# One encoder step on one core: the router without a wait, half of the table products behind the first experts, later weight loads, squares summed on TensorE

## Chip, core and metric

The kernel runs on one core of a Trainium2 chip. The metric is device time in microseconds; the median of three runs of the kernel before is 1087.63 us (1087.05 to 1094.18). TensorE is called PE below, VectorE DVE, ScalarE ACT, GpSimd POOL, and SP is the engine that only issues transfers. DMA stands for the transfer engines.

## What is computed

Two layers over 288 tokens (256 of a prompt, 32 of a running stream) of width 1024, all in float32. Layer 0 mixes with RWKV-7, layer 1 with forgetting attention. Each layer has two norms, so there are norms 0 to 3; after norm 0 and norm 2 comes the mixture of 16 experts, top 2 for each token, which is where the change lies:

```python
x = _layer_norm(ALPHA * x + gt1 * y, ln_g[l, 0], ln_b[l, 0])      # norm 0, norm 2
h = x * (1 + sc2) + sh2
gl = h @ rg_w + rg_b;  el = h @ re_w + re_b                       # router
gsel = argmax(gl);  top_v, top_i = top_k(el[gsel], 2)
comb = weights of the two chosen experts
hid = silu(h @ wg[e]) * (h @ wu[e]) * comb;  y = sum_e hid @ wd[e]
x = _layer_norm(ALPHA * x + gt2 * y, ln_g[l, 1], ln_b[l, 1])      # norm 1, norm 3
```

`_layer_norm` takes mean and variance over the 1024 features. The conditioning (`sh`, `sc`, `gt`) is a product of a small vector with a 1024 x 6144 matrix for each layer ("ada").

## The kernel before, in words

Activations lie with features on the partitions, as 8 tiles of 128 x 288. There is no scheduler: each engine's program is written out by hand, with waits on named counters (semaphores) between the engines, and each engine takes its instructions strictly in order.

**A norm** (`residual` and `layer_norm`). For each of the 8 tiles DVE adds the gated sub-layer output to ALPHA * x (L1400) and adds the result into a running sum `zsum_` (L1392, L1394). ACT squares the tile (L1852), POOL sums the squares into `ssum` (L2073). PE multiplies `zsum_`, then the last tile, by a matrix of 1/1024 (L853, L855: the mean on all partitions) and does the same with `ssum` and the last squares (L858, L860). DVE centres the tiles (L1410), makes 1/std (L1419 to L1421, ACT's square root), and multiplies each tile (L1428). In norms 0 and 2 ACT and POOL make the router's input `Hh` from that (L1866, L2079), and POOL then makes x itself (L2082), counted by `x_ready`; DVE's `layer_norm` ends with a wait for all of x. In norms 1 and 3 ACT makes x (L1862).

**The router** (`moe`). PE forms 20 logits per token (L869) and transposes them (L582); DVE finds the group, the two experts and their weights in some 40 small instructions (L1438 to L1499), with two exponentials from ACT (L1883, L1885) on the way. ACT also copies the transposed `Hh` and sends it to DRAM (`hbuf`).

**The tables.** For each group g of four experts, `select(g)` on DVE (L1506) makes a 0/1 matrix, and 96 / 4 = 24 small PE products (L904) turn it into a table of rows per expert: 64 slots with token row, output row and weight. DVE copies tables from PSUM (`table`, L1516), counted by `tbl_ready`, and POOL gathers each expert's tokens from `hbuf` with an indirect transfer (`fetch`, L2101). PE also counts the tokens of each expert (L892, `cnt_mm`). Six indirect transfers (`places`, L2093) write a second table for experts with over 64 tokens, which a loop takes after the 16 ("overflow" jobs, two in each layer here).

**The experts.** For expert e PE transposes the gathered rows (`step_t`), multiplies by gate and up weights (`step_u`, L919), transposes the hidden rows (`step_h`), and multiplies by the down weights (`step_d`, L930). The order is T0, then for each e: T(e+1), U(e), D(e-1), H(e). The weights are 3 MB per expert in four slots; SP issues gate/up of expert e+4 (L510) once U(e) is done and down of e+4 (L514) once D(e) is. POOL sends each result to DRAM (`zbuf`, L2106), ACT loads the rows back for both choices (`zin`, L1927), DVE adds them (L1626), and PE transposes them for the norm.

**Next weights.** In layer 0 SP issues, behind the last expert loads, the first half of the key weights (`half(4, 0)`), three of the four 2 MB pieces of the third ada turn (`ada_weights(3, j)`), then the rest once the rows are back. PE runs three ada pieces (`ada_slot`, L616) between the overflow loop and the transposes, the fourth in the key projection (`project(4)`, L595).

## Times and profile before

| | us |
|---|---|
| median of 3 runs | 1087.63 |
| profiled execution | 1085.29 |
| its span (first to last instruction) | 1083.7 |
| PE busy in the span | 886.5 (82%) |
| chain that ended last, on PE | 60% |
| chain that ended last, on DMA | 21% |

The rows below come from that one profiled execution. A time like 420.86 is in us from the start of the span. "Idle before <-X" in brackets is the time that the engine stood before the instruction, and what ended it. PEclk is the granted clock of TensorE as a share of 2.4 GHz; 0.50 is 1.2 GHz.

### The profile page before, as it was taken

How to read it: one execution, taken by the hardware profiler on the slowest of the kernel's cores; microseconds unless marked ns; L12 is line 12 of the kernel's file. 1: busy time of each engine (PE TensorE's matmuls, PEld its weight loads, DVE VectorE, ACT ScalarE, POOL GpSimd, SP SyncE). 2: the span in 40 equal slices, each digit the busy share in tenths (PEclk: the TensorE clock that was granted, in tenths of full speed). 3: DMA queues.
4: the chain of work that ended last, by engine and by line, in shares of the span. 5: the costliest groups of instructions: out<-in, count | busy, mean ns of one | idle time of the engine just before them, and what ended most of it. 6: DMA issues, size and time to landing. Idle time of an engine off the chain costs nothing.

```text
span 1083.7 us, 19216 instructions
## 1 busy us (share of the span) xinstructions
PE 886.5 (82%) x8282; PEld 597.1 (55%) x8282; DVE 336.0 (31%) x849; ACT 234.3 (22%) x519; POOL 173.7 (16%) x216
## 2 busy tenths in 40 slices
PE   2799999899886877889875599898899778997742
PEld 0477667789764547545431377455367565454321
DVE  0522333445334544311112601231121542121126
ACT  0321225233212231111000423221222321110004
POOL 0100003020100032443111300000000234431122
PEclk9899989999997886899987699899899968999865
DMA  9642222330447501699997435355637315999831
GB/s 387 296 155 78 77 78 89 116 123 4 168 158 318 208 30 66 228 414 421 427 423 280 169 149 194 161 217 211 238 154 305 165 57 191 415 418 426 342 97 51
DMA packets 28997, 230.47 MB, mean 213 GB/s; under 512 B 7216, under 2 KB 7632, under 8 KB 14288
## 3 DMA queue, kind: packets, MB, share of 16 engines
q1 hardware_dynamic: 16704, 203.95, 46.7%
q0 software_dynamic: 8576, 15.83, 4.1%
q10 hardware_dynamic: 3632, 9.47, 2.6%
q8 instruction: 66, 1.08, 0.4%
q14 instruction: 19, 0.16, 0.0%
HBM read 223.21 MB, written 16.32 MB: 221 GB/s over the span
## 4 chain that ended last, share of the span: by engine, by line
PE 60%; DMA 21%; DVE 8%; issue 4%; ACT 2%; another core or an unknown queue 2%; SPq 1%; ACTq 1%; POOL 0%; DVEq 0%; POOLq 0%
PE ps L595 21%; DMA arena<-in_experts 8%; PE ps L919 8%; DMA arena<-in_w 8%; PE ps L721 5%; PE ps L616 4%; PE ps L930 3%; PE ps L728 3%; PE ps L904 3%; PE ps L582 3%; DMA ring<-in_w 2%; PE ps L1050 1%; DMA arena<-zbuf 1%; PE ps L734 1%
## 5 line engine op out<-in xcount | busy, mean ns | idle before, releaser
L595 PE MATMUL ps<-arena,ring 128*128 128x288 f32 x896 | 231.5, 421 | 13.8 <-DVE arena L1379 4.9
L595 PEld LDWEIGHTS ps<-arena,ring 128*128 128x128 f32 x896 | 173.8, 197 | 71.2 <-issue 16.9
L919 PE MATMUL ps<-arena 128*64 128x256 f32 x1152 | 149.9, 419 | 25.0 <-DMA arena<-in_experts 24.8
L919 PEld LDWEIGHTS ps<-arena 128*64 128x64 f32 x1152 | 87.9, 151 | 78.7 <-issue 27.4
L582 PE MATMUL ps<-con,arena 128*128 128x128 f32 (+3 forms) x254 | 52.5, 321 | 40.0 <-DVEq L1629 19.0
L582 PEld LDWEIGHTS ps<-con,arena 128*128 128x128 f32 (+3 forms) x254 | 32.1, 153 | 86.6 <-issue 37.8
L616 PE MATMUL ps<-arena,csil 128*32 128x512 f32 x256 | 40.8, 768 | 43.5 <-DMA arena<-in_w 42.4
L930 PE MATMUL ps<-arena 128*64 128x512 f32 x288 | 67.8, 593 | 1.6 <-DVE arena L1579 1.6
L1576 DVE TENSOR_TENSOR arena<-arena,ps 128x128 f32<-128x128 f32 x36 | 10.4, 288 | 184.2 <-ACT arena L1892 176.2
L721 PE MATMUL ps<-arena 64*64 64x64 f32 x1888 | 63.8, 221 | 4.5 <-issue 3.7
L721 PEld LDWEIGHTS ps<-arena 64*64 64x64 f32 x1888 | 60.7, 138 | 10.1 <-issue 8.4
L2106 POOL DMA_INDIRECT zbuf<-arena,TBL x32 | 32.3, 1008 | 133.8 <-DVE arena L1583 119.3
L1892 ACT ACTIVATE arena<-ps 128x128 f32<-128x128 f32 x36 | 10.0, 278 | 170.8 <-PE ps L919 144.1
L616 PEld LDWEIGHTS ps<-arena,csil 128*32 128x32 f32 x256 | 7.9, 126 | 66.7 <-DMA arena<-in_w 33.5
L1889 ACT ACTIVATE arena<-ps 128x512 f32<-128x512 f32 x36 | 21.3, 597 | 104.8 <-PE ps L582 104.8
L1823 ACT ACTIVATE arena<-ps 128x512 f32<-128x512 f32 x44 | 26.2, 597 | 79.6 <-PE ps L721 59.2
L1760 ACT ACTIVATE arena<-ps 128x288 f32<-128x288 f32 x40 | 16.2, 409 | 123.9 <-PE ps L595 123.8
L1852 ACT ACTIVATE arena<-arena 128x288 f32<-128x288 f32 x32 | 14.2, 443 | 125.2 <-DVEq L1404 125.2
L2101 POOL DMA_INDIRECT ring<-hbuf,TBL x32 | 33.0, 1030 | 39.8 <-DVEq L1519 30.7
L930 PEld LDWEIGHTS ps<-arena 128*64 128x64 f32 x288 | 20.7, 137 | 27.9 <-issue 21.4
L1211 DVE SCALAR_TENSOR_TENSOR arena<-arena,vec 128x288 f32<-128x288 f32 x48 | 21.6, 516 | 45.0 <-PE ps L595 43.9
L1583 DVE TENSOR_SCALAR arena<-ps,TBL 128x512 f32<-128x512 f32 x32 | 24.0, 750 | 34.0 <-PE ps L930 33.1
(292 smaller groups left out, 1140.0 us busy)
## 6 DMA issues: line engine op xcount, KB each, us to landing
arena<-in_experts SPq DMA_DIRECT2D x32, 2048.0 KB
ring<-in_w SPq DMA_DIRECT2D x24, 2048.0 KB, 8.3
arena<-in_w SPq DMA_DIRECT2D x16, 2048.0 KB, 12.9
arena<-in_experts SPq DMA_DIRECT2D x32, 1024.0 KB
arena<-in_experts SPq DMA_DIRECT2D x4, 3072.0 KB, 19.4
arena<-zbuf ACTq DMA_DIRECT2D x8, 512.0 KB, 5.9
arena<-in_lora SPq DMA_DIRECT2D x1, 2560.0 KB, 40.5
hbuf<-arena ACTq DMA_DIRECT2D x4, 512.0 KB, 3.2
```

Of the source, the lines that this page charges most:

```text
L582: return nc.tensor.transpose(out, in_, ident[0:n, 0:n])
L595: last = mm(ps[:, tile % 4, 0:T], wslot[j][:, k, o * P:(o + 1) * P], rhs_at(k), start=k == 0, stop=k == KT - 1)
L616: last = mm(ps[32 * q:32 * q + 32, ADA_BANK[turn], :], c2[:, 2 * j + k, :], w[:, k, q, :], start=j == 0 and k == 0, stop=j == ADA_TURN - 1 ...
L721: last = mm(o, lhs[r, k, :], rhs[r, k, :], start=True, stop=True)
L728: last = mm(ps[r, bank, k * 64:(k + 1) * 64], lhs[r, k, :], rhs[r, k, :], start=n == 0, stop=n == len(terms) - 1)
L904: last = mm(ps[r, 6 if g == 0 else 7, 4 * e:4 * e + 3], sel[0:n, i, e4, :], val[0:n, i, e, :], start=i == 0, stop=i == 2)
L919: last = mm(ps[64 * j:64 * j + 64, 2 + b, 0:256], xselT[b][:, o:o + C], ewgu[slot][:, k, j * 256:(j + 1) * 256], start=k == 0, stop=k == K ...
L930: last = mm(ps[64 * n:64 * n + 64, 4 + b, :], hidT[b][:, f * C:(f + 1) * C], ewd[slot][:, f, n * 512:(n + 1) * 512], start=f == 0, stop=f ...
L1583: return V.tensor_scalar(y, ps[:, 4 + b, :], w.bitcast(F32), None, ALU.mult)
L1823: ins = Ac(B[dst], src, ACT.Copy, scale=-1.0 if product == "Bt" else 1.0)
L2101: Pl.indirect_dma_start(out=x, out_offset=None, in_=hbuf[layer], in_offset=bass.IndirectOffsetOnAxis(ap=idx, axis=0), bounds_check=2 * T - ...
L2106: Pl.indirect_dma_start(out=zbuf[layer], out_offset=bass.IndirectOffsetOnAxis(ap=idx, axis=0), in_=y, in_offset=None, bounds_check=4 * T - ...
```

## The change

- **Router.** DVE's wait for x moves from the end of `layer_norm` to just before `select(0)`, and DVE clears the router's tiles while it waits for the mean. The buffers of `SEL` and of the squares (`SQB`) move for that.
- **Tables.** PE makes tables 0, then the counts, then tables 1; tables 2 go behind U0 and tables 3 behind U1. DVE copies each group's table by itself, and POOL waits for the third and fourth before it gathers experts 8 and 12.
- **Norms 1 and 3.** PE takes the squares of each tile as they come (`add_squares`, one product per tile between the transposes), and POOL instead of DVE sums the tiles.
- **All norms.** POOL centres tiles 5 to 7 (`OWN`).
- **Next weights.** SP waits until the rows are back (`z_in0`, `z_in1`) before it issues `half(4, 0)`; all four ada pieces come after `half(4, 1)`, and PE takes them one by one inside the key projection. The load of `fw` goes from the middle of layer 0's experts to their end, and POOL's loads for attention wait for the ada pieces.

```diff
+OWN = 5
...
-        fw = cut(2 * ACOL + 6 * D, KT * 80)
...
+        fw = er[0][:, WCOL:WCOL + KT * 80]
...
-        ZB, SQB = (4, 5, 4, 5), (5, 1, 5, 1)
+        ZB, SQB = (4, 5, 4, 5), (3, 1, 3, 1)
...
             moe_loads(0)
+            for h in range(2):
+                sp.wait_ge(s[f"z_in{h}"], 48)
             half(4, 0)
-            sp.wait_ge(s["dn_mm"], NE)
-            for j in range(ADA_TURN - 1):
-                ada_weights(3, j)
-            sp.wait_ge(s["zsum"], 2)
             sp.wait_ge(s["o_over"], 2)
             half(4, 1)
-            ada_weights(3, ADA_TURN - 1)
+            for j in range(ADA_TURN):
+                ada_weights(3, j)
             for n in range(10, 14):
...
+                if n % 2:
+                    add_squares(n, KT - 2)
                 pe.wait_ge(s["ln_sum"], n + 1)
                 mm(ps[:, 4, 0:T], co("mean"), zsum_, start=True, stop=False)
                 pe.wait_ge(s["z_ready"], KT * (n + 1))
                 mm(ps[:, 4, 0:T], co("mean"), acts(ZB[n])[:, KT - 1, :], start=False, stop=True)\
                     .then_inc(s["ln_mean"], 1)
-                pe.wait_ge(s["ln_ssum"], n + 1)
-                mm(ps[:, 5, 0:T], co("mean"), ssum, start=True, stop=False)
-                pe.wait_ge(s["ln_sq"], KT * (n + 1))
-                mm(ps[:, 5, 0:T], co("mean"), acts(SQB[n])[:, KT - 1, :], start=False, stop=True)\
-                    .then_inc(s["ln_var"], 1)
+                if not n % 2:
+                    pe.wait_ge(s["ln_ssum"], n // 2 + 1)
+                    mm(ps[:, 5, 0:T], co("mean"), ssum, start=True, stop=False)
+                add_squares(n, KT - 1).then_inc(s["ln_var"], 1)
+            def add_squares(n, k):
+                pe.wait_ge(s["ln_sq"], KT * n + k + 1)
+                return mm(ps[:, 5, 0:T], co("mean"), acts(SQB[n])[:, k, :], start=k == 0, stop=k == KT - 1)
...
                 pe.wait_ge(s["ht_evac"], 6 * (layer + 1))
-                for i, n in enumerate(TOK):
-                    last = mm(ps[:, 6, 448:464], ones[0:n, :], mask[0:n, i, :], start=i == 0, stop=i == 2)
-                last.then_inc(s["cnt_mm"], 1)
                 val = VAL[:].rearrange("p (i e c) -> p i e c", i=NTT, e=NE)
-                for g in range(4):
+                def tables(g):
                     pe.wait_ge(s["sel_ready"], 4 * layer + g + 1)
                     sel = SEL[g % 2].rearrange("p (i e j) -> p i e j", i=NTT, e=4)
                     for e4 in range(4):
                         e = 4 * g + e4
                         for i, n in enumerate(TOK):
                             for r in HALF:
-                                last = mm(ps[r, 6 if g == 0 else 7, 4 * e:4 * e + 3], sel[0:n, i, e4, :],
+                                last = mm(ps[r, 6 + g % 2, 4 * e:4 * e + 3], sel[0:n, i, e4, :],
                                           val[0:n, i, e, :], start=i == 0, stop=i == 2)
                     last.then_inc(s["sel_mm"], 1)
+                tables(0)
+                for i, n in enumerate(TOK):
+                    last = mm(ps[:, 7, 448:464], ones[0:n, :], mask[0:n, i, :], start=i == 0, stop=i == 2)
+                last.then_inc(s["cnt_mm"], 1)
+                tables(1)
...
                     step_u(e)
+                    if e < 2:
+                        tables(2 + e)
                     if e:
                         step_d(e - 1)
                     step_h(e)
...
-                if layer == 0:
-                    for j in range(ADA_TURN - 1):
-                        ada_slot(3, j)
                 for k in range(KT):
...
+                    if k > 1:
+                        add_squares(2 * layer + 1, k - 2)
...
-                if tile == 2:
-                    ada_slot(3, ADA_TURN - 1)
-                if tile == 3:
+                if tile < ADA_TURN:
+                    ada_slot(3, tile)
+                if tile == 4:
                     ada_columns(3)
...
             def scaled_x(n):
+                if n:
+                    dve.wait_ge(s["x_ready"], KT * n)
                 link(V.tensor_scalar(act_flat(ZB[n]), act_flat(A_X), ALPHA, None, ALU.mult))
             def residual(n, layer, comp, tiles, freed, first):
...
-                    if k == 2:
-                        did(V.tensor_tensor(zsum_, Z[:, 0, :], Z[:, 1, :], ALU.add))
-                    elif k > 2:
-                        did(V.tensor_tensor(zsum_, zsum_, Z[:, k - 1, :], ALU.add))
-                    if k == KT - 1:
-                        settle()
-                        dve.sem_inc(s["ln_sum"], 1)
+                    if k > 1 and not n % 2:
+                        did(V.tensor_tensor(zsum_, Z[:, 0, :] if k == 2 else zsum_, Z[:, k - 1, :], ALU.add))
+                        if k == KT - 1:
+                            settle()
+                            dve.sem_inc(s["ln_sum"], 1)
                     dve.wait_ge(tiles, first + k + 1)
...
+                    dve.wait_ge(s["ln_sq"], KT * n + 1)
+                    for x in (LG, RT, JI[n // 2][:]):
+                        did(V.memset(x, 0))
...
-                    if k + 2 < KT:
+                    if k + 2 < OWN:
                         center(k + 2)
-                    ch.until(cent[k])
                     if k == 0:
                         dve.wait_ge(s["ln_rstd"], n + 1)
+                    if k < OWN:
+                        ch.until(cent[k])
+                    else:
+                        dve.wait_ge(s["ln_cent"], (KT - OWN) * n + k - OWN + 1)
                     V.tensor_tensor(Z[:, k, :], Z[:, k, :], lnr, ALU.mult).then_inc(s["u_ready"], 1)
-                dve.wait_ge(s["x_ready"], KT * (n + 1))
             def moe(layer):
...
-                did(V.memset(LG, 0.0))
-                did(V.memset(RT, 0.0))
-                did(V.memset(JI[layer][:], 0))
...
-                def table(g, a, b):
-                    dve.wait_ge(s["sel_mm"], 4 * layer + g)
-                    t4, p4 = (x.rearrange("p (e c) -> p e c", c=4)[:, a:b, :]
-                              for x in (TBL[:], ps[:, 6 if a == 0 else 7, 0:64]))
+                def table(g):
+                    dve.wait_ge(s["sel_mm"], 4 * layer + g + 1)
...
+                dve.wait_ge(s["x_ready"], KT * (2 * layer + 1))
                 select(0)
                 select(1)
-                table(1, 0, 4)
+                table(0)
                 select(2)
+                table(1)
                 select(3)
                 link(V.tensor_tensor(posE, place, bc(cE, 1, [P, NTT, NE]), ALU.add))
-                table(4, 4, NE)
                 dve.wait_ge(s["cnt_mm"], layer + 1)
-                did(V.tensor_copy(JT[0:1, 7, 0:16], ps[0:1, 6, 448:464]))
+                did(V.tensor_copy(JT[0:1, 7, 0:16], ps[0:1, 7, 448:464]))
...
+                        table(2 + e)
...
+                total, x, ready, done = (zsum_, Z, "z_ready", "ln_sum") if n % 2 else (ssum, Q, "ln_sq", "ln_ssum")
                 for k in range(1, KT - 1):
-                    pool.wait_ge(s["ln_sq"], KT * n + k + 1)
-                    ch.link(Pl.tensor_tensor(ssum, Q[:, 0, :] if k == 1 else ssum, Q[:, k, :], ALU.add))
-                pool.sem_inc(s["ln_ssum"], 1)
+                    pool.wait_ge(s[ready], KT * n + k + 1)
+                    ch.link(Pl.tensor_tensor(total, x[:, 0, :] if k == 1 else total, x[:, k, :], ALU.add))
+                pool.sem_inc(s[done], 1)
+                pool.wait_ge(s["ln_mu"], n + 1)
+                pool.wait_ge(s["ln_sq"], KT * (n + 1))
+                for k in range(OWN, KT):
+                    Pl.tensor_tensor(Z[:, k, :], Z[:, k, :], lnmu, ALU.subtract).then_inc(s["ln_cent"], 1)
...
-                pool.wait_ge(s["tbl_ready"], 2 * layer + 1)
+                pool.wait_ge(s["tbl_ready"], 4 * layer + 1)
                 for e in range(NSLOT):
                     fetch(e)
                 places()
-                if layer == 0:
-                    Pl.dma_start(fw, I["fw"]).then_inc(s["fw_in"], 16)
-                pool.wait_ge(s["tbl_ready"], 2 * layer + 2)
+                pool.wait_ge(s["tbl_ready"], 4 * layer + 2)
...
+                        if (e + NSLOT + 2) % 4 == 0:
+                            pool.wait_ge(s["tbl_ready"], 4 * layer + (e + NSLOT + 2) // 4 + 1)
...
+            Pl.dma_start(fw, I["fw"]).then_inc(s["fw_in"], 16)
             layer_norm(1)
-            pool.wait_ge(s["x_ready"], 2 * KT)
+            pool.wait_ge(s["ada_done"], 4 * ADA_TURN)
```

What this makes of the order on PE at the start of the experts (L582 `con,ring` is T, L919 U, L582 `con,arena` H, L930 D; L904, and L908 in the changed kernel, are the table products). Before:

```order
L892 MATMUL ps<-arena,con 128x16 x3
L904 MATMUL ps<-VAL,arena 64x3 x96
L582 MATMUL ps<-con,ring 128x128 x8
L919 MATMUL ps<-arena 64x256 x16
L582 MATMUL ps<-con,arena 128x128
L582 MATMUL ps<-con,ring 128x128 x4
L919 MATMUL ps<-arena 64x256 x16
L930 MATMUL ps<-arena 64x512 x4
```

Changed:

```order
L908 MATMUL ps<-VAL,arena 64x3 x24
L914 MATMUL ps<-arena,con 128x16 x3
L908 MATMUL ps<-VAL,arena 64x3 x24
L582 MATMUL ps<-con,ring 128x128 x8
L929 MATMUL ps<-arena 64x256 x16
L908 MATMUL ps<-VAL,arena 64x3 x24
L582 MATMUL ps<-con,arena 128x128
L582 MATMUL ps<-con,ring 128x128 x4
L929 MATMUL ps<-arena 64x256 x16
L908 MATMUL ps<-VAL,arena 64x3 x24
L940 MATMUL ps<-arena 64x512 x4
```

Half of the 96 products now stand behind U0 and U1.

The order on SP behind layer 0's experts (`ring<-in_w` is half a projection's weights, `arena<-in_w` an ada piece). Before:

```order
L472 DMA ring<-in_w 128x4096 [waits tile_done]
L481 DMA arena<-in_w 128x4096 [waits dn_mm]
L481 DMA arena<-in_w 128x4096 x2
L472 DMA ring<-in_w 128x4096 [waits tile_done,o_over,zsum]
L481 DMA arena<-in_w 128x4096
```

Changed:

```order
L473 DMA ring<-in_w 128x4096 [waits tile_done,z_in1,z_in0]
L473 DMA ring<-in_w 128x4096 [waits tile_done,o_over]
L482 DMA arena<-in_w 128x4096 x4
```

The first load now waits for the rows, and the ada pieces stand behind both halves.

## Rows read from the trace of the kernel before

**Rows 1.** Chain of waits, times 350 to 620: start us, us, what.

```profile
419.36 1.50 PE ps L892 x6
420.86 13.79 PE ps L904 x192
```

**Rows 2.** Timeline, layer 0 router: start, us, engine, line, instruction, [idle before, releaser].

```profile
410.03 0.11 DVE L1433 MEMSET arena<- 128x60 f32 x1 [6.07 <-POOL arena L2082]
...
414.81 0.21 ACT L1883 ACTIVATE arena<-arena 128x12 f32<-128x12 f32 x1
...
416.54 0.17 DVE L1483 TENSOR_REDUCE arena<-arena 128x3 f32<-128x12 f32 x1
...
419.47 0.21 DVE L1499 SCALAR_TENSOR_TENSOR arena<-ps,arena 128x48 f32<-128x48 f32 x1 [0.90 <-PE ps L888]
...
425.52 1.12 POOL L2101 DMA_INDIRECT ring<-hbuf,TBL  x1 [15.57 <-DVEq L1519]
```

**Rows 3.** Timeline, layer 1 router.

```profile
878.26 0.21 ACT L1883 ACTIVATE arena<-arena 128x12 f32<-128x12 f32 x1
...
879.28 0.17 DVE L1483 TENSOR_REDUCE arena<-arena 128x3 f32<-128x12 f32 x1
...
881.80 0.21 DVE L1499 SCALAR_TENSOR_TENSOR arena<-ps,arena 128x48 f32<-128x48 f32 x1 [0.49 <-PE ps L888]
```

**Rows 4.** Windows: stretch, length, busy PE, PEld, DVE, ACT, POOL; PEclk, DMA share, GB/s.

```profile
430.00:432.00 2.00, 2.00 (x26) 1.86 (x24) 0.00 (x0) 0.00 (x0) 0.60 (x1) 0.50 0.56 155
438.00:440.00 2.00, 2.00 (x16) 1.14 (x14) 1.79 (x7) 0.47 (x1) 1.66 (x2) 0.65 0.02 2
452.00:564.00 112.00, 95.81 (x673) 51.71 (x671) 18.63 (x46) 13.02 (x30) 29.64 (x31) 0.95 1.01 418
```

**Rows 5.** Timeline of SP's queue, layer 0: first expert loads behind the preloaded four.

```profile
442.26 0.33 SPq L510 DMA_DIRECT2D arena<-in_experts  x1
450.99 0.33 SPq L514 DMA_DIRECT2D arena<-in_experts  x1
...
459.37 0.33 SPq L514 DMA_DIRECT2D arena<-in_experts  x1
...
465.39 0.33 SPq L514 DMA_DIRECT2D arena<-in_experts  x1
```

**Rows 6.** The same in layer 1.

```profile
903.81 0.33 SPq L510 DMA_DIRECT2D arena<-in_experts  x1
913.29 0.33 SPq L514 DMA_DIRECT2D arena<-in_experts  x1
```

**Rows 7.** Waits: who waited for what, us in total, times, longest.

```profile
ACT arena L1892 <- remote: 26.7, 4, 7.0
```

**Rows 8.** Timeline, end of layer 0's expert stage.

```profile
575.98 1.92 PE L616 MATMUL ps<-arena,csil 128*32 128x512 f32 x16 [1.07 <-DVE arena L1583]
...
576.56 1.38 POOL L2106 DMA_INDIRECT zbuf<-arena,IDXJ  x1 [0.66 <-issue]
...
584.78 3.02 ACTq L1927 DMA_DIRECT2D arena<-zbuf  x6
```

**Rows 9.** Timeline, end of layer 1's expert stage and its last norm.

```profile
1040.28 1.38 POOL L2106 DMA_INDIRECT zbuf<-arena,IDXJ  x1 [0.65 <-issue]
1044.14 3.18 ACTq L1927 DMA_DIRECT2D arena<-zbuf  x6
...
1060.45 0.93 PE L582 MATMUL ps<-con,arena 128*128 128x128 f32 x3 [0.32 <-DVEq L1403]
...
1061.83 1.04 DVE L1394 TENSOR_TENSOR lnw<-lnw,arena 128x288 f32<-128x288 f32 x1 [0.24 <-DVE arena L1400]
...
1065.49 1.33 PE L853 MATMUL ps<-lnw,con 128*128 128x288 f32 x2 [4.11 <-DVEq L1397]
...
1069.81 0.46 DVE L1419 SCALAR_TENSOR_TENSOR lnw<-ps,lnw 128x288 f32<-128x288 f32 x1 [0.72 <-PE ps L860]
...
1073.67 5.35 ACT L1862 ACTIVATE arena<-arena,vec 128x288 f32<-128x288 f32 x8 [0.60 <-DVE arena L1428]
```

More of the change, by code:

```diff
@@ L394, in build @@
         assert ARENA - 512 - NSLOT * ECOL >= 6 * ACOL and ARENA - 512 - ECOL >= 14 * ACOL
+        fw = er[0][:, WCOL:WCOL + KT * 80]
         ewgu = [e[:, 0:WCOL].rearrange("p (k n) -> p k n", k=KT) for e in er]
         ewd = [e[:, WCOL:ECOL].rearrange("p (f n) -> p f n", f=2) for e in er]
-        at = [2 * ACOL]
-        SEL = [take(NTT * 4 * C) for _ in range(2)]
+        at = [2 * ACOL + 2 * NTT * 4 * C]
         htok = take(3 * D).rearrange("p (i d) -> p i d", i=3)
@@ L412, in build @@
         hsil, hid, hidT = ([take(P) for _ in range(2)] for _ in range(3))
+        SEL = [take(NTT * 4 * C) for _ in range(2)]
         assert at[0] <= 5 * ACOL
@@ L1605, in moe @@
                     step_h(e)
+                    if e < 2:
+                        table(2 + e)
                 step_d(NE - 1)
```

5 lines of the change are left out of this document (4 added, 1 removed).

## The prediction

> **What bounds the kernel now.** I read the chain of waits first. It says which stages hold the end, and around the change it goes through PE until the experts begin: [rows 1] show the counts on PE and then 192 table instructions (96 products) in 13.79 us, 3.45 us for each of the four groups. The timeline shows what stands before them. In layer 0 DVE stands 6.07 us, released by POOL's last tile of x [rows 2]. Next I read the windows of the expert stage. From 452 to 564 us the DMA engines are busy at a share of 1.01 and move 418 GB/s [rows 4]: the stage behind the first experts is bound by weight transfers, not by PE, although PE is busy 95.81 of 112 us. Its end is therefore its start plus a fixed number of bytes. The start is the first gate/up load behind the four preloaded experts, which SP issues when U0 is done: 442.26 us [rows 5] and 903.81 us [rows 6]. SP's next load waits for D0, 8.73 and 9.48 us later; 2 MB take some 5 us at 418 GB/s, so part of that gap is an idle DMA queue and counts as well. A microsecond won before U0 is a microsecond of the whole; one won inside the saturated part is nothing.
>
> **Router.** Taking out the wait cannot give 6.07 us, because ACT is late next. In layer 0 the first exponential runs at 414.81 us [rows 2], behind the evacuations and the sending of `hbuf` on the same engine, which do not move. The second can follow at about 415.05 and DVE's L1483 at about 415.3 instead of 416.54: 1.2 us. Behind L1483 DVE also lost 0.90 us to PE's positions before L1499 at 419.47 [rows 2]; these now start earlier with the mask, so that goes too: **2.1 us** in layer 0. In layer 1 the exponential is at 878.26, so L1483 moves from 879.28 to about 878.7, and the 0.49 us before L1499 goes [rows 3]: **1.0 us**. The clearing of tiles on DVE (under 1 us) falls into the wait for the mean. x itself is ready at 410.03 at the latest, and `select(0)` comes some 7 us later, so the moved wait costs nothing. If the exponentials should not bind, up to 6.07 us would be the other end.
>
> **Tables.** Before U0 stand now tables 0, the counts (1.50 us [rows 1], formerly made while DVE was still busy, now on the path) and tables 1: 3.45 + 1.5 + 3.45 = 8.4 us instead of 13.8, a gain of 5.4 us. The gathers limit this. The first is issued at 425.52 [rows 2], four stand 1.35 us apart, and gather traffic is at its height (155 GB/s) at 430 to 432 us [rows 4]; I take 4.3 us from issue to landing (between 3.5 and the 9 us at which PE used it). DVE's copy of table 0 still waits for tables 0 alone, so the gather moves up only by the router's gain and lands at about 427.7, half a microsecond after PE is ready; the second costs PE another 0.3. U0 gains 2.1 + 5.4 - 0.8 = **6.7 us** in layer 0 and 1.0 + 5.4 - 0.1 = **6.3 us** in layer 1.
>
> The moved half comes back in part. D0 now stands behind both late groups. The cadence of experts is 6.0 us (459.37 to 465.39 [rows 5]), the clock there is 1.00, and at that clock I take a group at half of 3.45 us, 1.72, since all of [rows 1] ran at 0.50. From U0 to D0 that makes 6.0 + 2 x 1.75 = 9.5 us, against 8.73 and 9.48 before. Those already held a late signal of PE, for which ACT and SP stood (the four "remote" waits, 6.7 us each [rows 7], twice what the products in them need; each comes while POOL issues indirect transfers back to back). In the new order D0 is due at about the end of POOL's issues, so I count no such wait on top. Cost: 0.8 us in layer 0, nothing in layer 1. Later copies of tables on DVE (0.3 us each) and POOL's waits before experts 8 and 12 are hidden behind a DMA-bound stage; its backlog is what covers them. **Experts together: -5.9 - 6.3 = -12.2 us.**
>
> **Centring on POOL.** In all four norms POOL's three subtractions start with DVE's first two. When a POOL operation overlaps a DVE one with two SBUF operands, the latter takes 1.04 us (L1394 at 1061.83 [rows 9]) where an operation of its size like L1419 takes 0.46. If DVE's second centring waits once, 1/std starts 0.2 to 0.9 us later. The Trainium skill speaks against this part of the change: SBUF — State Buffer, section "SBUF: two separate sides", says that DVE (with two SBUF inputs) and GpSimd share a port pair as an exclusive lock held for a whole instruction, and the loser stands still. By that rule each norm would pay one POOL subtraction. From the row I take +0.4 us per norm. The gain is in the last tiles: ACT's 8 outputs take 5.35 us in the last norm [rows 9], paced by DVE's alternation of two operations per tile; with three fewer it should be 0.9 us less, which counts at the very end only, since behind norm 1 PE is slower than its supply. Four norms: +1.6 - 0.9 = **+0.7 us** (ends: -1 and +4).
>
> **Norms 1 and 3.** DVE loses six sums of 0.46 us. PE gains six products of 288 columns, and they stand in front of the next transposes. At 1.2 GHz three transposes take 0.93 us and a pair of means 1.33 us for the first [rows 9], so a tile costs PE about 1.9 us, more than DVE's 1.22 before (three tiles from 1061.83 to L853 at 1065.49); stepped through tile by tile the variance comes 2.2 us later than the 1069.81 of [rows 9]. At 2.4 GHz it comes 2.3 us earlier. PE would now work without a pause for some 10 us, where before it stood 4.11 us ahead of L853 [rows 9]; in the experts the clock rose in the window at 438 us, some 4 us after dense work began [rows 4]. I take a rise midway: **-1.0 us per norm, -2.0** (ends -4.6 and +4.4).
>
> **Next weights.** In layer 0 the last scatter (issued 576.56) was followed by ACT's loads at 584.78, in layer 1, with no weights in the queue, 1040.28 by 1044.14 [rows 8, 9]: 8.22 against 3.86 us. With the loads held back layer 0 should do as layer 1: **-4.4 us**, and 0.2 on the rows. The first half of the key weights then has some 19 us until the projection and needs 8; the second waits for the overflow's last gathers, as before, and is needed 16 us into it. But three ada pieces that PE ran while it waited now stand inside the projection, where PE is the bound: 3 x 1.92 us [rows 8] = **+5.7 us**. Their four transfers (about 5 us each) come before the piece is wanted. POOL's loads for attention start some 15 us later, with 45 us left. Together **+1.1 us**: this part alone is a loss.
>
> **Sum.** -12.2 + 0.7 - 2.0 + 1.1 = -12.4 us against the profiled execution's own 1085.29: 1072.9. That execution lies 2.3 us under the median of 1087.63, so I forecast 1075.2 as a median, 12.4 us or 1.1% less. About 1% (10.9 us, 1076.7) is what a measurement of this kernel tells from no change.
>
> **Rivals.**
>
> - *The late table products pull the clock down (ends slower).* For: in 430 to 432 us PE was busy 2.00 of 2.00 us with table products and still at 0.50 [rows 4], and it stayed there until dense work had run for 4 us. Against: a group would last only 1.7 us. If the clock fell behind U0, U0 to D0 would be 2 x 3.45 + 2 x 6.0 = 18.9 us in place of 9.5, 9.4 us lost per layer; with both layers the sum is +6.4 us, 1094. It makes the kernel slower as soon as the gap from U0 to D0 passes about 15.7 us in both layers. With one spell of 4 us per layer at half rate it is 4 us lost, 1079. The Trainium skill (TensorE: Matmul & The Clock Gate, "What's actually happening") says that the throttled state is the default and activity releases it. By that rule alone tables on a fully busy PE would release it; the row says they did not, so the rule does not protect the moved half.
> - *POOL's transfers hold PE's signal at U0.* The four gathers now come 3 us before the six scatters. If that is one burst of the kind in [rows 7], U0's signal comes with its end, about 5.5 us late in each layer: 1075.2 + 11 = 1086.
> - *PE stays at 1.2 GHz in the odd norms and the port costs its full price:* 4.4 + 2.0 + 2.0 more, 1083.
> - *More than forecast:* the clock holds through tables 0 and 1, because PE's pause before the positions is shorter. Then they take half and the gathers bind: 2 to 4 us per layer, 1069.
>
> **Chances.** Forecast 0.50 (own range 1070 to 1080), clock 0.15, burst 0.17, norms 0.08, more 0.10. All but a fifth lies between 1067 and 1088: the low end is the better case with some of the bounds, the high end the burst. Faster by over 1%: 0.38 of the forecast's 0.50, the better case, and a little of the rivals, 0.50. Slower by over 1% needs the clock rival beyond its full bound or a stall that no row shows: 0.06. The rest, 0.44, is within 1%.
>
> **What the new profile would show.** DVE's 6 us wait gone, L1483's counterpart held by ACT. The first expert load on SP earlier by 6.7 and 6.3 us, counted from the end of the norm before it, and the next one 9.5 us behind it. DMA saturated from then on, with the same bytes. ACT's load of rows 4 us behind the last scatter in both layers. The key projection 5.7 us longer. In norms 1 and 3 the granted clock decides the sign. The prediction is wrong if U0 to D0 passes 13 us, if U0's signal comes well behind its last product, or if the saturated stretch gets longer.

## The result and the profile after

| | before | after |
|---|---|---|
| median of 20 runs, us | 1087.09 | 1096.18 |
| profiled execution, us | 1085.29 | 1095.14 |
| its span, us | 1083.7 | 1093.5 |

The ratio is 1.0064, with a 95% interval from 1.0045 to 1.0083: 0.6% slower, where 1.1% faster was forecast, and outside the range. Both traces, cut at the same events, give:

| stretch | before | after | difference | forecast |
|---|---|---|---|---|
| start to the projection ahead of norm 0 | 357.84 | 357.68 | -0.2 | 0 |
| to U0's load on SP, layer 0 | 84.42 | 78.70 | -5.7 | -6.3 |
| U0 to D0 | 8.73 | 15.62 | **+6.9** | +0.8 |
| to the key projection | 164.45 | 161.11 | -3.3 | -5.2 |
| key projection | 40.06 | 45.53 | +5.5 | +5.7 |
| next projection and attention | 168.77 | 171.83 | +3.1 | 0 |
| to U0's load, layer 1 | 79.54 | 74.75 | -4.8 | -5.9 |
| U0 to D0 | 9.48 | 17.39 | **+7.9** | 0 |
| to the end | 170.41 | 170.89 | +0.5 | -1.5 |

(The forecast's column puts its 0.4 us a norm for the port into the stretch that holds the norm.) The two gaps cost 14.8 us, and 0.8 was forecast. In the same view as [rows 5, 6], SP's queue:

```profile
436.38 0.33 SPq L511 DMA_DIRECT2D arena<-in_experts  x1
452.00 0.33 SPq L515 DMA_DIRECT2D arena<-in_experts  x1
...
458.02 0.33 SPq L515 DMA_DIRECT2D arena<-in_experts  x1
...
905.22 0.33 SPq L511 DMA_DIRECT2D arena<-in_experts  x1
922.61 0.33 SPq L515 DMA_DIRECT2D arena<-in_experts  x1
```

From D1 on the cadence is 6.02 us, as before. PE's timeline between the first two of these rows (L908 is a table product, L582 a transpose, L929 gate/up, L940 down):

```profile
436.17 1.92 PE L908 MATMUL ps<-VAL,arena 128*64 128x3 f32 x41
438.94 0.59 PE L908 MATMUL ps<-VAL,arena 128*64 128x3 f32 x6 [0.86 <-issue]
440.38 0.16 PE L908 MATMUL ps<-VAL,arena 32*64 32x3 f32 x1 [0.85 <-issue]
440.47 0.47 PE L582 MATMUL ps<-con,arena 128*128 128x128 f32 x1
440.74 1.06 PE L582 MATMUL ps<-con,ring 128*128 128x128 f32 x4
441.82 2.55 PE L929 MATMUL ps<-arena 128*64 128x256 f32 x8
444.66 3.43 PE L929 MATMUL ps<-arena 128*64 128x256 f32 x24 [0.28 <-issue]
447.86 2.23 PE L908 MATMUL ps<-VAL,arena 128*64 128x3 f32 x48
450.02 1.94 PE L940 MATMUL ps<-arena 128*64 128x512 f32 x8
```

PE stops three times for nothing that the profile shows ("issue"), and U1 takes 6.3 us where an expert's gate/up takes 3.67 at full clock. Meanwhile POOL issues transfers, and ACT waits for a PE signal that comes only after POOL's last one (timelines of POOL and ACT; L2117 scatters places, L2125 gathers tokens):

```profile
433.31 1.03 POOL L2117 DMA_INDIRECT tbl<-ENT,SLOT  x1 [4.93 <-DVEq L1557]
...
442.30 1.01 POOL L2125 DMA_INDIRECT ring<-hbuf,TBL  x1 [0.31 <-issue]
445.65 1.00 POOL L2125 DMA_INDIRECT ring<-hbuf,TBL  x1 [2.33 <-remote]
```
```profile
444.92 0.60 ACT L1907 ACTIVATE arena<-ps 128x512 f32<-128x512 f32 x1 [8.25 <-remote]
```

The transposes that ACT waited for ended near 441.8; POOL's burst of eight ended at 443.3. The windows, with the columns of [rows 4]:

```profile
442.00:444.00 2.00, 1.88 (x8) 0.49 (x8) 0.00 (x0) 0.00 (x0) 1.01 (x1) 0.50 0.58 225
444.00:446.00 2.00, 1.72 (x10) 1.25 (x10) 0.50 (x3) 0.60 (x1) 0.35 (x1) 0.52 0.15 41
446.00:448.00 2.00, 2.00 (x25) 1.84 (x23) 0.00 (x0) 0.00 (x0) 0.65 (x1) 1.00 0.28 60
448.00:450.00 2.00, 2.00 (x50) 1.88 (x45) 0.29 (x1) 0.28 (x1) 0.00 (x0) 1.00 0.08 32
450.00:452.00 2.00, 2.00 (x13) 0.60 (x11) 0.00 (x0) 0.00 (x0) 0.00 (x0) 1.00 0.04 8
452.00:564.00 112.00, 96.13 (x675) 51.79 (x675) 19.50 (x48) 13.05 (x30) 29.54 (x31) 0.95 0.98 407
```

For the last 8 us of the gap the DMA engines stand nearly still (shares 0.15, 0.28, 0.08, 0.04) and afterwards they are full: nothing wins the gap back. PE's rows fill the gap with no wait for ACT or DVE in them: the late signal is a sign of the trouble, but PE itself, stopped and slow, sets the 15.62 us. Two things meet here, a clock of 0.50 and a PE that is held up; the trace alone can't say which of them makes the gap.

### The profile page after: what moved, and what is told of

Its sections match the earlier page's. It is cut to its first block, busy times and chain, and to the rows that moved or that the text cites. A ratio compares the mean times of both kernels' runs of the same rounds, so it can differ in the third digit from the quotient of the medians.

```text
span 1093.5 us, 19272 instructions
## 1 busy us (share of the span) xinstructions
PE 893.0 (82%) x8306; PEld 598.5 (55%) x8306; DVE 329.7 (30%) x833; ACT 233.0 (21%) x519; POOL 183.0 (17%) x228
## 4 chain that ended last, share of the span: by engine, by line
PE 60%; DMA 24%; DVE 5%; issue 4%; ACT 3%; POOL 1%; another core or an unknown queue 1%; SPq 1%; ACTq 1%; POOLq 0%; DVEq 0%
PE ps L595 20%; DMA arena<-in_experts 10%; PE ps L929 7%; DMA arena<-in_w 7%; PE ps L721 5%; PE ps L616 4%; PE ps L728 3%; PE ps L582 3%; PE ps L940 3%; PE ps L908 2%; PE ps L1061 2%; DMA ring<-in_w 2%; DMA IDXJ<-tbl 1%; PE ps L734 1%; PE ps L875 1%
## 5 line engine op out<-in xcount | busy, mean ns | idle before, releaser
L929 PE MATMUL ps<-arena 128*64 128x256 f32 x1152 | 154.7, 425 | 28.1 <-DMA arena<-in_experts 24.7
L929 PEld LDWEIGHTS ps<-arena 128*64 128x64 f32 x1152 | 91.5, 153 | 83.3 <-issue 31.0
L582 PE MATMUL ps<-con,arena 128*128 128x128 f32 (+3 forms) x254 | 51.5, 316 | 34.1 <-DVEq L1647 27.5
L582 PEld LDWEIGHTS ps<-con,arena 128*128 128x128 f32 (+3 forms) x254 | 33.3, 153 | 82.9 <-issue 40.4
L940 PE MATMUL ps<-arena 128*64 128x512 f32 x288 | 67.9, 594 | 1.6 <-DVE arena L1595 1.6
L1778 ACT ACTIVATE arena<-ps 128x288 f32<-128x288 f32 x40 | 16.2, 409 | 123.2 <-PE ps L595 123.2
L2125 POOL DMA_INDIRECT ring<-hbuf,TBL x32 | 32.9, 1029 | 42.2 <-DVEq L1534 28.2
L1411 DVE SCALAR_TENSOR_TENSOR arena<-ps,mod,arena 128x256 f32<-128x256 f32 x64 | 20.6, 363 | 53.9 <-PE ps L595 43.0
L940 PEld LDWEIGHTS ps<-arena 128*64 128x64 f32 x288 | 20.5, 137 | 27.7 <-issue 21.4
```

The lines of the kernel that those rows point to most:

```text
L582: return nc.tensor.transpose(out, in_, ident[0:n, 0:n])
L929: last = mm(ps[64 * j:64 * j + 64, 2 + b, 0:256], xselT[b][:, o:o + C], ewgu[slot][:, k, j * 256:(j + 1) * 256], start=k == 0, stop=k == K ...
L940: last = mm(ps[64 * n:64 * n + 64, 4 + b, :], hidT[b][:, f * C:(f + 1) * C], ewd[slot][:, f, n * 512:(n + 1) * 512], start=f == 0, stop=f ...
L2125: Pl.indirect_dma_start(out=x, out_offset=None, in_=hbuf[layer], in_offset=bass.IndirectOffsetOnAxis(ap=idx, axis=0), bounds_check=2 * T - ...
```

## Experiments

Four edits to the changed kernel, all around the gap, ran first, on one chip; the kernel before beside them has a median of 1086.83 us. Each run left one profiled execution.

**Places later.** POOL's six scatters leave the place in front of the gathers of experts 4 and 5.

```diff
-                places()
...
+                    if e == 4:
+                        places()
-                    if e == 2:
+                    if e == 6:
                         pool.wait_ge(s["tbl_scat"], 96 * (layer + 1))
```

> The changed kernel with POOL's six scatters of places moved from in front of the gathers of experts 4 and 5 to behind the sending of expert 3, and the wait for them with the first overflow gathers to expert 6. The table products stay where the change put them. Burst theory (POOL's back-to-back indirect transfers hold the signals between engines and stop PE): the burst now ends some 7.5 us earlier, before U0's products are done, so U0 to D0 falls from 15.6 and 17.4 us to 9.5 to 11, the stops of PE inside tables 2 and the remote waits of 7 to 8 us at U0 go, and the median falls by about 12 us to 1084. Clock theory (the late products drop PE to 1.2 GHz and that alone makes the gap): U0 to D0 stays at 14 us or more and the median stays within 3 us of 1096.

Median 1082.14 us, ratio to the kernel before 0.9965 (0.9945 to 0.9984). By the medians that is 14 us under the changed kernel, by the two ratios, each taken beside its own runs of the kernel before, about 11 us. The gaps are 11.89 and 10.79 us. PE's timeline, layer 0, and two windows:

```profile
436.54 2.19 PE L908 MATMUL ps<-VAL,arena 128*64 128x3 f32 x48
438.66 0.33 PE L582 MATMUL ps<-con,arena 128*128 128x128 f32 x1
438.83 0.60 PE L582 MATMUL ps<-con,ring 128*128 128x128 f32 x4
439.36 5.36 PE L929 MATMUL ps<-arena 128*64 128x256 f32 x32
444.55 2.18 PE L908 MATMUL ps<-VAL,arena 128*64 128x3 f32 x48
446.66 1.94 PE L940 MATMUL ps<-arena 128*64 128x512 f32 x8
```
```profile
438.00:440.00 2.00, 2.00 (x25) 1.59 (x27) 0.56 (x4) 0.54 (x1) 0.00 (x0) 0.86 0.69 270
440.00:442.00 2.00, 2.00 (x13) 1.06 (x12) 0.00 (x0) 0.06 (x1) 1.00 (x1) 0.50 0.97 418
```

The stops are gone, and so is the late signal at U0. They went with the burst: its scatters now stand at 469.56 us and later, and there ACT waits for U5:

```profile
482.59 0.28 ACT L1910 ACTIVATE arena<-ps 128x128 f32<-128x128 f32 x1 [8.04 <-remote]
```

There the weights' queue is full: two D stand 9.97 us apart instead of 6.02, but the whole stretch from D0 to the key projection is only 1.9 us longer than in the changed kernel (163.04 against 161.11). So the burst theory holds for the larger part. It doesn't hold for all: the gap missed its 9.5 to 11 in layer 0, because U1 took 5.36 us at a clock that fell although PE was busy 2.00 of 2.00 us.

**Tables later.** Groups 2 and 3 behind H1 and H2, places where the change has them.

```diff
-                    if e < 2:
-                        tables(2 + e)
                     if e:
                         step_d(e - 1)
                     step_h(e)
+                    if e in (1, 2):
+                        tables(1 + e)
```

> The changed kernel with table products 2 and 3 put on PE behind H1 and H2 (DVE's copies with them), so behind D0 and D1; POOL's order stays. Burst theory: the burst of POOL still holds U0's signal to about 444.5 us, H0 comes behind that, and the gap U0 to D0 is 9 to 11 us; median about 1085. Clock theory: with no small products behind U0 the clock stays up and the gap is 8.7 us or less, with ACT and DVE still waiting no more than 4 us for U0; median about 1081. If neither tables nor burst but something else behind U0 makes the gap, it stays at 15 us.

Median 1096.81 us, ratio 1.0084 (1.0057 to 1.0111). The gaps are 9.83 and 10.20 us, in the burst theory's range, but the median is neither theory's: the next two D come 13.04 and 10.01 us apart instead of 6.02. In layer 0 the signal of U1 comes late to ACT, during and just behind POOL's nine issues, and PE itself waits 3.09 us for what follows from it. But PE does not stop inside its products this time: U1 takes its usual 3.67 us and D0 1.89 while POOL issues. Behind that wait the tables run at half clock (ACT, then PE):

```profile
447.08 0.28 ACT L1910 ACTIVATE arena<-ps 128x128 f32<-128x128 f32 x1 [7.12 <-remote]
```
```profile
448.14 3.40 PE L908 MATMUL ps<-VAL,arena 128*64 128x3 f32 x48
451.47 1.11 PE L582 MATMUL ps<-con,ring 128*128 128x128 f32 x4
452.52 5.92 PE L929 MATMUL ps<-arena 128*64 128x256 f32 x32
```

So the gap alone does not tell the two causes apart: moving either of them out shortens it. The time does: it falls when the burst goes, and not when only the tables go, because burst and tables then cost two experts later.

**Both later.** The two edits together.

> Both moves at once: scatters of places behind expert 3, table products 2 and 3 behind H1 and H2. Burst theory: nothing of either stands between U0 and D0; the gap is the bare cadence, 6 to 7.5 us, and the median falls to about 1077. Clock theory: the same as with the tables late alone, 1081. If the loads then find the DMA queue idle for another reason (the gathers of expert 1), the gap stays above 9 us.

Median 1080.84 us, ratio 0.9950 (0.9923 to 0.9977), not told apart from places later alone. The gaps are 9.05 and 7.90 us, above the burst theory's 6 to 7.5. The surplus in layer 0 is neither burst nor tables. PE stands for DVE, whose small instructions for the second table run until 440.3 us and come ahead of what H0 needs:

```profile
440.95 0.33 PE L582 MATMUL ps<-con,arena 128*128 128x128 f32 x1 [2.95 <-DVE arena L1592]
```

The wait is 2.95 us in layer 0 and 1.81 in layer 1; without it both gaps are 6.1 us, the bare cadence. D1 and D2 follow 9.94 and 9.96 us apart in layer 0. After each late group the clock reads low there with PE busy all the time (windows behind the first):

```profile
448.00:450.00 2.00, 2.00 (x37) 1.90 (x36) 0.05 (x2) 0.00 (x0) 1.03 (x1) 0.85 0.88 266
450.00:452.00 2.00, 2.00 (x11) 1.11 (x11) 0.28 (x2) 0.60 (x1) 0.71 (x1) 0.50 1.12 471
```

**All tables first.** On DVE the copies of groups 2 and 3 come behind `select(3)`.

```diff
                 tables(1)
+                tables(2)
+                tables(3)
...
                     step_u(e)
-                    if e < 2:
-                        tables(2 + e)
```

> The changed kernel with all four groups of table products in front of the first expert again; the rest of the change stays. U0 comes 6.9 us later in each layer (two groups of 3.45 us), U0 to D0 goes back to 8.7 to 9.5 us. Both theories: what the move won ahead of U0 it lost behind it, so the median is within 3 us of the changed kernel's 1096; the difference to the forecast then lies wholly in the gap. If it is under 1090, the move of the tables itself cost time.

Median 1090.62 us, ratio 1.0029 (1.0003 to 1.0054). U0 comes 6.4 and 5.3 us later, the gaps are 7.36 and 9.49. That is neither within 3 us of 1096 nor under 1090. By the trace the move of the tables won 11.7 us ahead of U0 and gave away 16.2 us in the two gaps, so it cost 4.5 us net; by the ratios (1.0064 and 1.0029) it is 4 us, with intervals that overlap.

The second group of runs was made on another chip, with its own runs of the kernel before beside it (median 1084.47 us). All but the last stand on places later, which itself did not run on that chip.

**Next weights as before.**

```diff
-            for h in range(2):
-                sp.wait_ge(s[f"z_in{h}"], 48)
             half(4, 0)
+            sp.wait_ge(s["dn_mm"], NE)
+            for j in range(ADA_TURN - 1):
+                ada_weights(3, j)
+            sp.wait_ge(s["zsum"], 2)
             sp.wait_ge(s["o_over"], 2)
             half(4, 1)
-            for j in range(ADA_TURN):
-                ada_weights(3, j)
+            ada_weights(3, ADA_TURN - 1)
...
+                if layer == 0:
+                    for j in range(ADA_TURN - 1):
+                        ada_slot(3, j)
...
-                if tile < ADA_TURN:
-                    ada_slot(3, tile)
-                if tile == 4:
+                if tile == 2:
+                    ada_slot(3, ADA_TURN - 1)
+                if tile == 3:
                     ada_columns(3)
```

> The kernel with places behind expert 3 (1082.1 us), and with the next weights as before the change: first half of the key weights and three ada pieces in the queue ahead of the rows, three ada pieces on PE ahead of the transposes, the fourth in tile 2 of the projection. As forecast (this part cost 1.1 us): ACT loads the rows 8 us instead of 3 behind the last scatter, the key projection is 5.5 us shorter, median about 1081. If the held-back loads also cost the attention stage its 3 us, the median is about 1078. If the rows' 5 us count in full and the projection's do not, 1086.

Median 1078.05 us, ratio 0.9929 (0.9902 to 0.9956). The projection takes 40.51 us, not 46, and D0 to the projection 166.45, not 160.7 to 163: what holding the loads back won it paid out again. Together the two are 206.96 us, against 206.87 and 207.32 in the next two runs. The median is that of the second branch by chance: the attention stretch, on which that branch rests, is 169.8 us, where places later has 169.2.

**Odd norms as before.**

```diff
-                if not n % 2:
-                    pe.wait_ge(s["ln_ssum"], n // 2 + 1)
-                    mm(ps[:, 5, 0:T], co("mean"), ssum, start=True, stop=False)
+                pe.wait_ge(s["ln_ssum"], n + 1)
+                mm(ps[:, 5, 0:T], co("mean"), ssum, start=True, stop=False)
...
-                    if k > 1:
-                        add_squares(2 * layer + 1, k - 2)
...
-                    if k > 1 and not n % 2:
+                    if k > 1:
                         did(V.tensor_tensor(zsum_, Z[:, 0, :] if k == 2 else zsum_, Z[:, k - 1, :], ALU.add))
...
-                total, x, ready, done = (zsum_, Z, "z_ready", "ln_sum") if n % 2 else (ssum, Q, "ln_sq", "ln_ssum")
+                total, x, ready, done = ssum, Q, "ln_sq", "ln_ssum"
```

> The kernel with places behind expert 3 (1082.1 us), with norms 1 and 3 summed as before: zsum on DVE while the tiles come, squares on POOL, one product for the squares. Theory 1 (PE at 1.2 GHz makes the squares dearer than DVE's sums in norm 3, POOL's late sum binds norm 1): norm 3's variance comes about 2 us earlier, norm 1's 1 to 3 us earlier, median 1078 to 1080. Theory 2 (forecast: the squares on PE save 1 us per norm): median about 1084.

Median 1077.34 us, ratio 0.9935 (0.9904 to 0.9966); D0 of layer 1 to the end is 168.24 us, 1.1 less than in the run above: from the first tile to 1/std norm 3 takes 13.5 us, where the run above takes 14.9. Norm 1 is no faster (15.9 us for 15.8). Its sum on POOL stands behind the overflow's gathers here too, and PE waits 1.93 us for it, as it waits 1.90 in places later.

**No centring on POOL.**

```diff
-OWN = 5
+OWN = 8
```

> The kernel with places behind expert 3 (1082.1 us), all centring on DVE, none on POOL. Theory 1 (the shared port holds DVE's first two centrings and the variance's chain): norms 0 and 2 are 0.6 to 0.8 us shorter each, norm 1 the same, the last norm's eight outputs 0.9 us longer, median 1081 to 1082. Theory 2 (POOL's centring saves more at the ends than the port costs): 1084.

Median 1076.44 us, ratio 0.9933 (0.9904 to 0.9962). DVE's first pair of centrings takes 0.83 us again instead of 1.42, and ACT's last eight outputs 5.35 instead of 4.69, as the first theory has it. The last stretch is 2.0 us shorter than in the first run of this group (167.38), but the larger part of that is the clock, which rose before the last two tiles of norm 3. The ratios of these three are all 0.3% under that of places later, whichever part was undone. In layer 0 all three, and the four runs further down, have a gap of 10.18 us and the clock at 1.00 behind the tables, with the same products on as busy a PE:

```profile
438.00:440.00 2.00, 2.00 (x22) 1.32 (x20) 0.00 (x0) 0.24 (x1) 0.99 (x1) 1.00 1.07 459
```

In layer 1 the seven gaps are 10.2 us three times and 12.6 four times, the latter with U1 at 5.36 us again. In these four PE stood 0.60 to 0.76 us for DVE just before the fall, in the other three it did not stand. None of the edits touches either place. The stretch before U0 in layer 0, which only the centring touches, is 76.1 to 76.8 us in the seven, 78.6 in places later. So the 0.3% cannot be put down to the edits. 10.2 us is the gap without burst and without a fall of the clock.

Something else is missing in these runs, and it bears on the main reading. The burst stands where places later has it, but no signal is late, in any of the eight traces of this group and the next. In the first run of this group POOL issues eleven indirect transfers in a row from 465.76 to 479.60 us, and in the middle of them ACT waits 3.02 us, as long as the products take (POOL, then ACT):

```profile
467.07 0.99 POOL L2122 DMA_INDIRECT tbl<-ENT,SLOT  x1 [0.30 <-issue]
...
478.61 0.99 POOL L2135 DMA_INDIRECT zbuf<-arena,TBL  x1 [0.30 <-issue]
```
```profile
474.52 0.28 ACT L1915 ACTIVATE arena<-ps 128x128 f32<-128x128 f32 x1 [3.02 <-PE ps L931]
```

In places later the same place cost ACT 8.04 us. The chip differs, the code there does not. So a burst alone does not make the stall. What else it takes is open, and the changed kernel itself was not run on these two chips.

**Kernel before, places later.** The next run is the kernel before with the first diff of this section.

> The kernel before, with one edit: the six scatters of places behind the sending of expert 3, the wait for them and the first overflow gathers at expert 6. Burst theory: the waits for PE's signals at U0 of 6.7 us (four) fall to the 3 us of the products or less, U0 to D0 falls from 8.73 and 9.48 to 6 to 7 us, median about 1082. If the kernel before hides its burst (the table products and the burst together are what hurts), median within 1.5 us of 1087.

Median 1082.81 us, ratio 0.9977 (0.9951 to 1.0004): unclear at this resolution. The gaps are 6.79 and 7.28 us, where the kernel before has 8.73 and 9.48, and none of the waits of [rows 7] is left; but no trace of the kernel before was taken on this chip, where no trace shows a stall by a burst. The kernel before's own trace shows what its burst cost. D0's products end at 449.01 us, and SP issues the load that waits for them at 450.99 [rows 5], 1 us behind POOL's last issue:

```profile
447.12 1.89 PE L930 MATMUL ps<-arena 128*64 128x512 f32 x8
```

That is 2.0 us of late signal in layer 0; in layer 1 it is 2.6 us (products until 910.65, load at 913.29 [rows 6]). So the burst cost the kernel before some 4 us in its gaps too, in that execution.

The last four ask how good a version can be. They ran on a third chip (kernel before beside them: 1081.76 us).

**Two ada pieces behind norm 1.** Shown is what is new in it; the loops over the pieces further on then start at 2.

```diff
             half(4, 0)
+            for j in range(2):
+                ada_weights(3, j)
             sp.wait_ge(s["o_over"], 2)
...
             layer_norm(1)
+            for j in range(2):
+                ada_slot(3, j)
```

> Places behind expert 3, all centring on DVE, norms 1 and 3 summed as before the change, and of the four ada pieces the first two loaded ahead of the overflow's last gathers and multiplied on PE right behind norm 1's variance, where PE stands some 5 us for DVE and ACT; pieces 2 and 3 stay in tiles 2 and 3 of the key projection. If PE's idle time behind the variance is free, the projection is 3.8 us shorter and starts on a running clock; median 12 us under the kernel before. If the two loads delay the gathers for which POOL waits ahead of its sums, norm 1 gives that back and the median is the next run's.

Median 1075.53 us, ratio 0.9922 (0.9892 to 0.9952), so 6 to 8 us and not 12. The projection fell to 41.0 us, but the second theory held as well: the gathers landed later, POOL summed later, and PE stood for it.

```profile
604.02 1.33 PE L861 MATMUL ps<-lnw,con 128*128 128x288 f32 x2 [7.35 <-POOLq L2091]
```

**POOL out of the odd norms.** The edit against the changed kernel, without what the run above shows:

```diff
-                    if k > 1 and not n % 2:
+                    if k > 1:
                         did(V.tensor_tensor(zsum_, Z[:, 0, :] if k == 2 else zsum_, Z[:, k - 1, :], ALU.add))
...
+                if not n % 2:
+                    for k in range(1, KT - 1):
+                        pool.wait_ge(s["ln_sq"], KT * n + k + 1)
...
+                    pool.sem_inc(s["ln_ssum"], 1)
```

> As the run above, but in norms 1 and 3 zsum is made on DVE and the squares are summed on PE, so POOL has no part in them and its wait for the overflow's last gathers stands in nobody's way. Norm 1's variance comes 2 to 4 us earlier than with POOL's sums; norm 3 is up to 2 us longer, PE at 1.2 GHz. Median 12 to 14 us under the kernel before; if PE's pace of 1.9 us a tile is the bound in both, no better than the run above.

Median 1072.33 us, ratio **0.9916** (0.9888 to 0.9943): the best point estimate of all, 9 us under the kernel before and short of the 12 to 14 expected. PE no longer waits for POOL; the variance is done at 597.2 us, and the two pieces fill PE's idle time:

```profile
598.10 1.92 PE L618 MATMUL ps<-arena,csil 128*32 128x512 f32 x16 [0.88 <-DMA arena<-in_w]
603.22 1.92 PE L618 MATMUL ps<-arena,csil 128*32 128x512 f32 x16 [3.20 <-DMA arena<-in_w]
605.07 11.91 PE L597 MATMUL ps<-arena,ring 128*128 128x288 f32 x48
```

The last two are combinations of edits shown above.

> Places behind expert 3, all centring on DVE, norms 1 and 3 summed as before the change; the next weights as in the change. The single undoings gave 0.3% each; if they add, the median is 8 to 10 us under the kernel before, if they were the chip's scatter, 5 us.

> As the run above, with the next weights as before the change too: what is left of the change is the router, the split tables and the places behind expert 3. If holding the loads back is a loss of 1 to 3 us, the median is 9 to 12 us under the kernel before; if a gain, 7.

1075.38 us, ratio 0.9948 (0.9925 to 0.9971), and 1075.54 us, 0.9928 (0.9904 to 0.9952). The intervals of all four overlap: what is shown is 0.5 to 0.8% under the kernel before, not their order. The first of these two came out near the 5 us of its second branch: the single undoings did not add. The second, 6 to 8 us under, is nearest to the branch in which holding the loads back is a gain, but its interval does not rule the other out.

## Why the prediction was wrong

**The step that failed** is "From U0 to D0 that makes 6.0 + 2 x 1.75 = 9.5 us", with the sentence behind it that counts no late signal on top. Measured: 15.62 and 17.39 us. In layer 0 the 6.1 us above 9.5 split, by PE's rows, into 2.2 us in tables 2 (4.4 us where the group takes 2.19 without the burst, 1.7 of it the two stops), 2.5 us in U1 and 0.7 in H0 and T2 (half clock and one stop), and 0.7 us that the same order still takes above 9.5 with no burst and a clock of 1.00 (10.18), because a group costs 2.2 us at full clock. The last is a wrong price: 1.72 was half of the 3.45 at half clock, but these products don't halve. Taking the burst out gave back 3.7 and 6.6 us, on one chip, and moving only the tables out shortened the gap as well, to 9.8 and 10.2 us: a gap of this length needs both. So the rivals were two halves of one case. "POOL's transfers hold PE's signal" had 0.17 and 1086 us, "the clock" 0.15 and up to 1094, and both came at once; neither had them together, so the stated high end of 1088 was too low. A kernel slower by over 1%, which had 0.06, did not come: the measured 0.6% falls under the 0.44 of "within 1%", though not by the path that the 0.44 stood for. The stall was in sight in [rows 7]. I reasoned that D0 would be due at the end of POOL's issues, and overlooked that PE itself, not only its listeners, can stand during a burst: 0.86, 0.85 and 0.28 us here. In the order before, where no small products stood beside the burst, it cost 2.0 and 2.6 us.

**Router: right.** The counterpart of L1483 was forecast for 415.3 and that of L1499 for 417.4; both hold, and ACT's exponentials are what is late next [rows 2]:

```profile
415.15 0.17 DVE L1498 TENSOR_REDUCE arena<-arena 128x3 f32<-128x12 f32 x1 [1.02 <-ACT arena L1903]
...
417.21 0.21 DVE L1514 SCALAR_TENSOR_TENSOR arena<-ps,arena 128x48 f32<-128x48 f32 x1
```

**Tables ahead of U0: right in kind.** The groups still take 3.40 us each at half clock, and U0 came 5.7 and 4.8 us earlier. Of the missing 0.6 us in layer 0, norm 0 holds 0.2 more than forecast (0.6 for 0.4). The rest lies before U0, where PE stood 1.05 us for ACT's copy while POOL issued its four gathers; the prediction had 0.8 there in all. In layer 1 the missing 1.1 us was not traced.

**Centring on POOL: right in sign, somewhat too small.** The first pair of centrings collides with POOL's first (norm 1, DVE and POOL):

```profile
607.11 1.42 DVE L1426 TENSOR_TENSOR arena<-arena,lnw 128x288 f32<-128x288 f32 x2 [6.81 <-ACT lnw L1872]
```
```profile
607.15 2.84 POOL L2098 TENSOR_TENSOR arena<-arena,lnw 128x288 f32<-128x288 f32 x3 [2.92 <-ACT lnw L1872]
```

The pair takes 0.83 us without POOL, so 0.6 us a norm is lost here, where 0.4 was taken. The gain at the end was 0.64 us (eight outputs in 4.71 us for 5.35 [rows 9]), where 0.9 was taken. The rule cited ahead of the result (the Trainium skill, SBUF — State Buffer, "SBUF: two separate sides") agrees in kind with this row: DVE loses most, though not all, of one POOL subtraction (2.84 / 3 = 0.95 us).

**Norms 1 and 3: wrong sign in both, by another bound in norm 1.** In norm 3 the clock stayed at 0.50 until the last squares, so PE's pace of 1.93 us a tile set the end: the case worked out at 1.2 GHz. From the first tile to 1/std it takes 16.1 us for 13.5, the forecast's +2.2 us for the variance and its 0.4 for the port; from the first tile to the end of the span it became 1.9 us longer. In norm 1 the same way takes 17.3 us for 13.4. There PE was ready, and POOL was late, its sum standing behind the wait for the overflow's gathers in its queue:

```profile
604.34 1.32 PE L856 MATMUL ps<-lnw,con 128*128 128x288 f32 x2 [3.56 <-POOLq L2094]
```

The prediction named nothing that stands ahead of POOL's new sum. The stretch gained 3.3 us and not 5.2 because two misses met: the first tile came 7.2 us earlier, where 4.6 was forecast, and the norm took 3.8 us longer.

**Next weights: the pieces right, the sum not.** ACT's loads came 3.0 us behind the last scatter, against 8.22 [rows 8] and 3.86 forecast; the projection became 5.5 us longer, 5.7 forecast, three pieces more of 1.92 us each. With the loads as before (the first run of the second group) the two stretches together are the same to 0.4 us, so the forecast loss of 1.1 us is not there. The last scatter, ACT's loads and one of the pieces:

```profile
576.55 1.37 POOL L2130 DMA_INDIRECT zbuf<-arena,IDXJ  x1 [0.66 <-issue]
```
```profile
579.55 3.06 ACTq L1945 DMA_DIRECT2D arena<-zbuf  x6
```
```profile
618.89 1.92 PE L616 MATMUL ps<-arena,csil 128*32 128x512 f32 x16
```

**The attention stretch** (+3.1 us) was not forecast, and no edit explains it. It is 169.2 us in places later and in the run with the odd norms as before, 171.8 us in tables later and in the run without POOL's centring, on the same two chips and with the same code there. With the weight loads as before it is 169.8 in one run and 172.2 in another. So neither the chip nor an edit sorts the lengths; with one profiled execution for each kernel, more cannot be said. Its cause is open.

**The saturated stretch** behaved as said: from D0's load to the last gate/up products that wait for weights it took 112.9 us against 113.2, and gave nothing and took nothing.

## What to carry to other kernels

Work that is moved behind the first transfer of a bandwidth-bound stage delays the second one in full; price it by that gap, not by the stage's average. Before anything moves next to an engine's burst of indirect transfers, look for late "remote" signals in the old trace: they mean the burst is already there, and part of it may be covered by what stands around it. Take such a trace on more than one chip: here the same burst stalled PE's listeners on one and on two others it did not. And when an engine takes over a sum, list what stands in its queue ahead of it.

## What the runs showed of the hardware

- In the traces of the kernel before, of the changed kernel and of the first group of runs, eight to ten indirect transfers on POOL, 1.3 us apart, go with PE signals that arrive 1.0 to 1.8 us behind the last of them. The late signals moved with the burst (ACT's wait of 8.25 us at 444.9 became one of 8.04 at 482.6). In the changed kernel, where small table products stand beside the burst, PE's issue also stops, for 0.28 to 1.16 us at a time; with the tables moved away it did not stop under the same burst (gate/up in 3.67 us). Two transfers per expert in the steady stage show none of it.
- In the eight traces of the second and third group, on two other chips, eleven such transfers in a row made no signal late. What the stall needs besides the burst is open. By which path POOL's work holds PE was not tried. The Trainium skill (SBUF — State Buffer, "SBUF: two separate sides") says that only the port pair shared by POOL and DVE causes contention on the engines' side; if that is so, the path is not SBUF's ports, and no run here shows which it is.
- A group of 48 table instructions with 3 columns takes 3.40 us at 1.2 GHz and 2.19 at 2.4 GHz.
- Behind such a group the clock fell to 0.50 for some 4 us in layer 0 of places later and of both later, with a PE that was busy all the time. In seven other runs, on the two other chips, the same instructions in layer 0 left it at 1.00. In layer 1 it fell in four of the seven, the four in which PE had just stood 0.60 to 0.76 us for DVE; in layer 1 of places later PE stood 0.52 us and the clock stayed. What decides stays open.
